# Gates and branch projections of a first block: channels by tokens against tokens by channels at 512 columns

## What is computed

```python
h = rms_norm(x, norm_w[layer])
proj = jnp.einsum('bsd,de->bse', h, w_in[layer])
...
ys = jnp.stack([y_a, y_b, y_c], axis=2)
branch = jnp.einsum('bsiw,iwd->bsid', ys, w_proj[layer])
g = jax.nn.sigmoid(gates.reshape(b, s, N_BRANCH, d) + gate_bias[layer])
merged = jnp.sum(g * branch, axis=2)
x = x + jnp.einsum('bsd,de->bse', merged, w_out[layer])
```

## Time and profile before

| | us |
|---|---|
| median of 3 runs | 2082.75 |
| lowest and highest | 2080.83, 2085.39 |
| the profiled execution | 2080.97 |
| its span, first to last instruction | 2079.3 |
| PE busy | 2054.9 (99%) |
| DVE busy | 1369.5 (66%) |
| ACT busy | 1100.1 (53%) |

### The profile page before, as it was taken

One profiled execution on the slowest core, in us unless ns is written; L12 is line 12 of the kernel. 1 busy time (PEld: TensorE's weight loads), 2 busy tenths in 40 slices (PEclk: granted clock), 3 DMA queues, 4 the chain that ended last, 5 costly groups with the idle time before them and its releaser, 6 DMA issues.

```text
span 2079.3 us, 36439 instructions
## 1 busy us (share of the span) xinstructions
PE 2054.9 (99%) x14782; PEld 1833.9 (88%) x14782; DVE 1369.5 (66%) x2356; ACT 1100.1 (53%) x1839; POOL 74.7 (4%) x55
## 2 busy tenths in 40 slices
PE   9999999999999999999999999999999999999998
PEld 9999999999999999997677887778888878999998
DVE  6787677566787777574464445665555666667786
ACT  5576676545676585553476233433332346645554
POOL 1311000000200000000000000000000000000000
PEclk9999999999999999999999999999999999999999
DMA  7545444567645445564222434433333343455552
GB/s 281 197 152 205 154 161 145 198 211 247 228 161 191 173 140 175 197 229 153 82 72 102 152 129 175 142 112 132 118 126 128 118 155 102 138 179 165 184 180 74
DMA packets 93512, 330.63 MB, mean 159 GB/s; under 512 B 10272, under 2 KB 13600, under 8 KB 93088
## 3 DMA queue, kind: packets, MB, share of 16 engines
q1 hardware_dynamic: 93344, 328.30, 46.3%
HBM read 327.08 MB, written 1.18 MB: 158 GB/s over the span
## 4 chain that ended last, share of the span: by engine, by line
PE 92%; DVE 4%; ACT 3%; issue 1%; DMA 0%; DVEq 0%; SPq 0%; ACTq 0%
PE ps L943 25%; PE ps L944 25%; PE ps L945 25%; PE ps L1026 2%; PE ps L956 1%; DVE t_lo L1682 1%; PE ps L957 1%; PE ps L958 1%; PE ps L1257 1%; ACT t_hi L1352 1%; PE ps L1278 1%; PE ps L1267 1%; PE ps L1099 1%; PE ps L1115 1%; PE ps L1080 1%
## 5 line engine op out<-in xcount | busy, mean ns | idle before, releaser
L943 PE MATMUL ps<-t_RB,t_hi 128*128 128x256 f32 (+1 forms) x3712 | 1163.4, 313 | 3.1 <-ACT t_MT L1398 1.4
L944 PE MATMUL ps<-t_RB,t_hi 128*128 128x256 f32 (+1 forms) x3712 | 1144.2, 308 | 0.0
L945 PE MATMUL ps<-t_RB,t_lo 128*128 128x256 f32 (+1 forms) x3712 | 1143.7, 308 | 0.0
L1682 DVE TENSOR_TENSOR t_lo<-t_raw,t_hi 128x1024 fp32r<-128x1024 f32 (+1 forms) x503 | 613.2, 1225 | 422.2 <-ACT t_hi L1352 417.0
L943 PEld LDWEIGHTS ps<-t_RB,t_hi 128*128 128x128 f32 x3712 | 707.8, 191 | 73.6 <-issue 27.6
L1352 ACT ACTIVATE t_hi<-t_raw 128x1024 fp32r<-128x1024 f32 (+1 forms) x506 | 524.6, 1042 | 437.2 <-PE ps L945 406.4
L944 PEld LDWEIGHTS ps<-t_RB,t_hi 128*128 128x128 f32 x3712 | 708.3, 191 | 35.1 <-issue 1.9
L945 PEld LDWEIGHTS ps<-t_RB,t_lo 128*128 128x128 f32 x3712 | 708.1, 191 | 35.1
L2122 DVE SCALAR_TENSOR_TENSOR t_A<-ps,t_V,t_A 128x510 f32<-128x510 f32 (+1 forms) x176 | 102.2, 612 | 90.1 <-ACT t_A L1642 88.5
L1642 ACT ACTIVATE t_A<-ps,t_V 128x512 f32<-128x512 f32 (+1 forms) x88 | 48.4, 576 | 127.3 <-PE ps L945 127.3
L2095 DVE SCALAR_TENSOR_TENSOR t_X<-ps,t_MOD,t_X 128x256 f32<-128x256 f32 x168 | 72.7, 477 | 35.2 <-PE ps L945 35.2
(11 more groups left out here) (304 smaller groups left out, 1902.6 us busy)
## 6 DMA issues: line engine op xcount, KB each, us to landing
t_raw<-in_W SPq DMA_DIRECT2D x586, 512.0 KB, 3.4
t_A<-cu_scratch SPq DMA_DIRECT2D x8, 512.0 KB, 5.8
t_B<-cu_scratch SPq DMA_DIRECT2D x8, 512.0 KB, 4.1
t_raw<-in_W SPq DMA_DIRECT2D x16, 256.0 KB, 2.7
t_A<-in_C SPq DMA_DIRECT2D x2, 1536.0 KB, 7.6
t_X<-in_X SPq DMA_DIRECT2D x2, 512.0 KB, 4.3
t_X<-in_X SPq DMA_DIRECT2D x1, 1024.0 KB, 7.8
out<-t_X SPq DMA_DIRECT2D x4, 256.0 KB, 2.5
```

Of the source, the lines that this page charges most:

```text
L943: mm(o, hi[:, w], xh(k), start=k == 0 and j == 0, stop=False)
L944: mm(o, hi[:, w], xl(k), start=False, stop=False)
L945: i = mm(o, lo[:, w], xh(k), start=False, stop=k == nkt - 1 and m == u.x[1] - 1)
L1682: tt(t.lo[s][:, 0:w], t.raw[r][:, 0:w], t.hi[s][:, 0:w].bitcast(F), ALU.subtract).then_inc(*up("dve", ("split", u.i)))
```

## The change

Gates and branch projections of the first block are turned round. The activations are now what is loaded into the array (128 tokens), and the split weights stream through it, 512 output channels per matmul (`tokens`). A chunk is four halves. A unit covers four of the eight steps `k` and both groups of 128 tokens, so 24 matmuls of 512 columns where there were 48 of 256, and it holds two banks of `gb`. Tokens lie on the partitions of the result. So the gate's bias lies along a row: `sync` fetches it, repeated to all partitions, into `RS` (12 transfers of 128 x 512 numbers), DVE adds it (a new operation), and ACT makes the sigmoid from SBUF. `MG` holds tokens by channels and has to be turned for `wout`: unit `mgt`, 8 transposes on PE, two copies on ACT into `HH`, two subtractions on DVE into `HL`, once for each half of the channels. The second one stands in the middle of the first two `wout` units, which now run side by side. `gn_sum` goes to the other pool of banks. Third, for every `gemm` of both networks, `split_after(i, 1)` moves behind `tick`. The number of halves and of `mod` units stays; a `mod` now waits for its turn over gate and projection units.

```diff
     def mod_turn(self):
         self.turn += 1
-        if self.every and self.turn % self.every == 0:
+        if self.every and self.turn >= self.every:
+            self.turn = 0
             self.some_mods(1)
+    def tok(self, kind, l, br, c, fn):
+        i, g = self.chunk(2 * CH, fn), (self.bank(), self.bank())
+        for h in range(2):
+            self.split_after(i, 2 * h)
+            self.add(kind, l=l, c=c, i=i, g=g, x=(h, 0, br))
+            self.tick()
+            self.split_after(i, 2 * h + 1)
+            self.turn += 1
...
-            elif last:
-                self.split_after(i, 1)
...
         if not urgent:
             self.tick()
+            self.split_after(i, 1)
             self.mod_turn()
...
-        gate(0)
-        gate(1)
-        proj(0)
-        gate(2)
+        def both(c):
+            cols = np.arange(c * 512, c * 512 + 512)
+            self.tok("gate", l, br, c, wcols("w_in", l, O_G + br * 1024 + cols))
+            if split and c:
+                self.add("mgt", l=l, c=0, s=(self.sbank(), self.sbank()))
+                if l == 1:
+                    self.side.append(self.context_norm())
+            self.tok("proj", l, br, c, wcols("w_proj", (l, br), cols, perm))
+        both(0)
         yield
...
+        both(1)
...
+        self.wide(l, [("wout", c, wout(c), 256, lambda m: (0, 2), None) for c in range(2)], 256, -1,
+                  (Unit("mgt", l=l, c=1, s=(self.sbank(), self.sbank()), led=True),))
...
+        if u.kind == "gate" and u.x[0] == 0:
+            br, old = u.x[2], {2: (), 0: (2, 1), 1: (0, 1)}[u.x[2]] if g == 0 else (u.x[2], 0)
+            q.wait_ge(at("gb", l, *old, 1) if old else at("smb", l))
+            src = t.d["GB"][(3 * l + br) * 2 + g].unsqueeze(0).to_broadcast([128, 512])
+            e.dma_start(t.RS[:, :], src).then_inc(*up("gbias", ("gbias", l, br, g), by=16))
...
+    def tokens(u, xh, xl, point, *events):
+        h = u.x[0]
+        for k in range(4 * h, 4 * h + 4):
+            q.wait_ge(point(k))
+            hi, lo = weights(u, k, 512)
+            for tb in range(2):
+                b, s = gbank(u, tb), slice(tb * 128, tb * 128 + 128)
+                mm(b[:, :], xh(k)[:, s], hi, start=k == 0, stop=False)
+                mm(b[:, :], xl(k)[:, s], hi, start=False, stop=False)
+                i = mm(b[:, :], xh(k)[:, s], lo, start=False, stop=k == 7)
...
+    def mgt(u):
+        for tb in range(2):
+            q.wait_ge(at("mg", u.l, 1, u.c, tb))
+            b = sbank(u, tb)
+            for j in range(4):
+                o = u.c * 512 + j * 128
+                i = e.transpose(b[:, j * 128:j * 128 + 128], t.MG[:, tb, o:o + 128], t.ident)
...
-        for m in range(2):
-            i = act(t.G[:, c % 2, m, :], b[:, m * 256:(m + 1) * 256], ACT.Sigmoid, bias=vec("gate_b", (l * 3 + br) * 8 + 2 * c + m))
+        h, _, br = u.x
+        for tb in range(2 * h):
+            q.wait_ge(at("gb", u.l, br, u.c, tb))
+            act(t.G[:, tb, :], t.G[:, tb, :], ACT.Sigmoid).then_inc(*up("act", ("gate", u.l, br, u.c, tb)))
...
+    def gate(u):
+        h, _, br = u.x
+        for tb in range(2 * h):
+            q.wait_ge(at("mm", u.i, tb), at("gbias", u.l, br, u.c), at("pvdone", "fox", u.l))
+            tt(t.G[:, tb, :], t.gb[u.g[tb] % 4][:, :], t.RS[:, :], ALU.add).then_inc(
+                *up("dve", ("gb", u.l, br, u.c, tb), ("gfree", u.g[tb])))
```

More of the change, by code:

```diff
@@ L302, in wide @@
                 group.append((Unit(kind, l=l, c=c, i=i, g=(self.bank(),), x=x(m0), led=True), then, m0))
-        self.add("wide", l=l, c=t, x=tuple(u for u, _, _ in group))
+        self.add("wide", l=l, c=t, n=mid, x=tuple(u for u, _, _ in group))
+        self.units += mid
         halves = [(i, h) for i in chunks for h in range(-(-self.width[i] // HF))]
@@ L482, in layer1 @@
             pass
-        self.add("msplit", l=l, c=3)
         self.tick()
@@ L487, in layer1, with wout @@
         self.side.append(self.squares(l + 1, PAIRED))
[L488 to L489 removed]
+        def wout(c):
+            return wcols("w_out", l, np.arange(c * 256, c * 256 + 256))
+        self.wide(l, [("wout", c, wout(c), 256, lambda m: (0, 2), None) for c in range(2)], 256, -1,
+                  (Unit("mgt", l=l, c=1, s=(self.sbank(), self.sbank()), led=True),))
+        self.tick()
+        self.tick()
+        for c in range(2, 4):
+            self.gemm("wout", l, c, wout(c), 8, 256, 256, urgent=c == 3)
         self.drain()
@@ L969, in wide @@
         idle(gbank(u.x[0]), u.c, 2)
-        for k in range(6):
+        for k in range(4 if u.n else 6):
             for v in u.x:
                 led[v.kind](v, ks=(k,))
+        for v in u.n:
+            mgt(v)
         for v in u.x:
-            led[v.kind](v, ks=(6, 7))
+            led[v.kind](v, ks=range(4 if u.n else 6, 8))
     def hh(k):
@@ L1307, in tensor @@
                 pair4=pair4, proj2=proj2, wout2=wout2, up=ffup, down=down)
-    led = dict(small=small, q=of_h, uf=uf, up=ffup, wout2=wout2)
+    led = dict(small=small, q=of_h, uf=uf, up=ffup, wout=wout, wout2=wout2)
     for u in units:
@@ L1528, in gn_sqrt, with mgt @@
         act(t.T1[:, 0:1024], t.T1[:, 0:1024], ACT.Sqrt, scale=1.0 / 256, bias=vec("small", 4)).then_inc(*up("act", ("gq", u.l)))
-    def msplit(u):
-        r = slice(2 * u.c, 2 * u.c + 2)
-        q.wait_ge(at("mg", u.l, 1, u.c), at("gatemm", u.l))
-        act(t.HH[:, r, :], t.MG[:, r, :], ACT.Copy).then_inc(*up("act", ("mh", u.l, u.c), ("m", u.l, u.c)))
+    def mgt(u):
+        l, c = u.l, u.c
+        for tb in range(2):
+            q.wait_ge(at("mgt", l, c, tb), at("gatemm", l))
+            act(t.HH[:, 4 * c:4 * c + 4, tb * 128:tb * 128 + 128], t.sb[u.s[tb] % 4][:, :].rearrange("p (k t) -> p k t", k=4),
+                ACT.Copy).then_inc(*up("act", ("mh", l, c, tb), *(("m", l, 4 * c + j) for j in range(4))))
     def rope(u):
@@ L2143, in vector @@
                 small4=small4, scores=scores, probs=probs, turn=turn, ssm0=ssm0, ssm1=ssm1, ssm1b=ssm1b, ssm2=ssm2, ssm4=ssm4, conv=conv, z=z,
-                ysplit=ysplit, gn=gn, proj=proj, msplit=msplit, rope2=rope2, wout=wout, s1=s1, norm2=norm2, pool1=mix1, four1=mix1,
+                ysplit=ysplit, gn=gn, gate=gate, proj=proj, mgt=mgt, rope2=rope2, wout=wout, s1=s1, norm2=norm2, pool1=mix1, four1=mix1,
                 mix2=mix2, rope2b=rope2b, pair0=pair0, pair2=pair2, pair3=pair3, pair4=pair4, proj2=proj2, msplit2=msplit2,
```

97 lines of the change are left out of this document (43 added, 54 removed).

## The result

The changed kernel takes 2091.11 us (median of 6 runs, 2089.43 to 2092.21), the kernel before in the same session 2083.03 (6 runs, 2080.83 to 2085.39). The ratio is 1.0041, with a 95% interval of 1.0030 to 1.0051: slower by some 8.5 us, where 7 less was forecast.

A forecast was written before the change was run, and what follows sets the result against it. PE, busy 99% of the span, was taken as the bound. Terms -15.4 + 3.6 + 3.5 - 2.9 - 2.0 + 6.0 = -7.2 against 2080.97 gave 2073.8, as a median 2075.5 us; range 2067 to 2083.

The forecast's parts named there:

- Part 1: Gates and projections: 48 units fall from 5.76 to 5.44 us each on PE, 15.4 us gained.
- part 2: The added mgt transposes, four times eight: 3.6 us more on PE (3.3 to 4.2).
- Part 3: End of each layer: PE idles 1.7 to 1.8 us behind the transposes within wout, 3.5 us in two layers.
- Part 4: Later split: shorter PE waits at the fox turn, 2.9 us gained, and in block 2, 2 us gained.
- Part 5: Third swa turn to pv: added DVE work makes PE wait 3.6 us, not 1.2; loss 6.0 us over both layers.
- costed at nothing: Bias transfers covered by 8 us of gate matmuls, additions hidden outside the swa stretch, sigmoids, banks and mod units: 0 us.
- DVE binds all gated stretches: Rival: bias additions and late splits cost PE their full time, 16.6 us, and Part 4 gains nothing; 2091 us, chance 0.08.

The follow-up runs named there:

- e12: e9 with matmuls on constants, which nothing reads, put into its longest PE waits; 2075.3 us, ratio 0.9971.
- e8: e3 with the second half's transposes behind two k of the two wout units in place of four; 2080.4 us, ratio 0.9991.
- e1: The kernel before with only the second half's split moved behind the side work; 2077.8 us, ratio 0.9982.
- e2: The changed kernel with every second half's split back ahead of the side work, so the new forms alone; 2097.2 us, ratio 1.007.
- e3: The changed kernel with each gate bias row fetched one projection earlier; 2084.0 us, ratio 1.001.
- e7: The changed kernel without the gate bias: no transfers, no additions, ACT's sigmoid reads PSUM; 2083.5 us, ratio 1.0007.
- e9: e3 plus gn 2 and 3 one unit later, three splits per layer on POOL, and tail transposes two k earlier; 2077.5 us, ratio 0.9978.

## Why the prediction was wrong, point by point

**Part 1, the matmuls, and part 2, the transposes: right.** A unit takes 5.44 us. The work of PE fell by 11.5 in the profile, by about 10.4 on average over all kernels with and without the forms, and by 9.4 in e12, where no fall blurs it, against 11.8. The Trainium skill's N / 2.4 + 2.5 ns per matmul ("TensorE: Matmul & The Clock Gate", "Back-to-back issue gap"), by which only 2.9 would have come, doesn't fit these matmuls: 240 ns for two of 256 columns and 227 for one of 512. The Trainium skill gives that formula, in the same section, for the isolated gap and says itself that in a stream of weight load and matmul both set the spacing; every matmul here has a weight load of its own, so the forecast was right to go by the rows.

**Part 3, the tail: right.** 1.57 us of idle PE in each layer, 3.1 in place of 3.5. e8 shows that it was avoidable.

**Part 4, the order: right in the fox attention, where the three waits went, and not shown in block 2.** e1 gained 4 us where 4.9 was forecast. Against it stand 1.6 of the 3.7 us behind layer 1. `pv` of the last fox group in layer 1, which had no wait, has one of 1.2 in the changed kernel; e2 has it (1.1) and e1 hasn't, so it comes with the forms.

**Part 5, the swa stretch: the mechanism and its size right, its surroundings wrong.** The 3.6 us of wait by DVE's volume are 4.0 in e3, where nothing else disturbs. In the changed kernel they are 4.7 to 5.7 (2.3 + 3.4 in layer 0, 2.3 + 2.4 in layer 1).

**The step that failed is in "costed at nothing".** It says that SP issues each bias transfer a quarter of a unit pair into the gate's matmuls, and that 8 us of matmuls cover it. The trace shows the issue 5 us after those matmuls had ended, because SP's queue waits in order and the load ahead of it waits for a split that DVE makes only behind `probs`, scores and `gn`, in the one stretch where DVE was behind. Part 4's late split adds 1.2 us to that, and is not the reason by itself: in e2 the issue is 4 us late without it. The landing, 4.8 us in the median of the twelve, wasn't priced either. The next sentence of that step even names what would follow, DVE standing at the addition with `turn` queued behind it, but prices it at nothing and puts PE's share "some 10 us later". It was some 6 us with what hung on it (e3), most of that through the clock.

**And one term was missing.** Nothing in the forecast or in its rivals lets the granted clock fall. The trace of before gave no cause to: it had 1.00 between start and end, but also no wait of PE above 1.4 us. The change made eight waits of 1.6 to 3.4 us, and six falls of 1.7 us came with them. The expected idle of part 5 and part 3 alone, 3.6 and 1.8 us at a time, was enough to ask what a wait of that length does to the clock. How much this and the rest weigh, e3 shows, where the transfer is out of the way: its profile is still 9.0 us above the forecast, 4.0 of them idle (it too has the new waits at the norm and the first pair), 3.5 clock and 1.5 work. So the late transfer alone explains less than half of the miss of some 16.

Of the rivals, the one that gave the measured time (DVE binds all gated stretches, 2091) had the wrong reason, as e7 and the 5.44 us spacing show.

## What to carry to other kernels

A new transfer takes the place in its queue that the code gives it: look at what the instruction ahead of it waits for, and on which engine that waits. On a kernel that keeps PE at 99%, price a new wait of PE at itself plus the chance of a clock fall (here 1.7 us, at times twice that), and count the work and the idle and the clock of the profile apart before explaining a difference. One profiled execution is a sample of one for falls, so read the granted clocks of the others beside it. Where a wait can't be removed, matmuls that nobody reads keep the clock up; that they gain time isn't shown, since e12's 2 us under e9 lie within the intervals. Try the halves of a change apart: here one half was worth 4 us and the other cost 15.
